# Eight of the sixteen gate tiles moved from the softmax loop to the linear attention

## The reference

```python
def mixer(z, w_in, ...):
    h = z @ w_in
    (q_a, k_a, v_a, r_a, lr_f, lr_b, q_b, k_b, v_b, g_a, g_b) = jnp.split(h, SPLIT_POINTS, axis=-1)
    a = gla_branch(q_a, k_a, v_a, r_a, lr_f, lr_b, ...)      # linear attention, 4 heads
    b = attention_branch(q_b, k_b, v_b, ...)                 # softmax attention, 8 heads
    y = (jax.nn.sigmoid(g_a + b_merge[0]) * (a @ w_pa)
         + jax.nn.sigmoid(g_b + b_merge[1]) * (b @ w_pb))
    return y @ w_out

# inside gla_branch, forward and on the flipped sequence, in chunks of 64 tokens:
    att = jnp.where(mask, jnp.einsum('bhnid,bhnjd->bhnij', q_dec, k_inv), 0.0)
    o_intra = jnp.einsum('bhnij,bhnjv->bhniv', att, vc)
    kv_chunk = jnp.einsum('bhnjd,bhnjv->bhndv', k_end, vc)   # state products
    ...                                                      # S = decay * S + kv_chunk
    o_inter = jnp.einsum('bhnid,bhndv->bhniv', q_dec, S_prev)
    ...
    o = o * lax.rsqrt(jnp.mean(o * o, axis=-1, keepdims=True) + EPS)   # group mean of each head
```

## Time and profile before

| | |
|---|---|
| runs shown | 3025.6 us median of 3 (3020.71 to 3026.71) |
| profiled execution | 3026.42 us, span 3024.6 us |
| PE matmul busy | 2682.4 us (89%), 18120 matmuls |
| PE weight load busy | 2040.7 us (67%) |
| DVE, ACT, POOL busy | 921.7, 911.7, 890.4 us (about 30% each) |
| mean granted TensorE clock | 0.941 |

### The profile page before, as it was taken

How to read it: one execution, slowest core, us unless ns; L and a number is a source line. 1 busy time by engine, 2 the same in 40 slices (tenths; PEclk the granted TensorE clock), 3 DMA queues, 4 the chain that set the end, 5 groups by cost and what they waited for, 6 DMA issues and landing times.

```text
span 3024.6 us, 44882 instructions
## 1 busy us (share of the span) xinstructions
PE 2682.4 (89%) x18120; PEld 2040.7 (67%) x18120; DVE 921.7 (30%) x2251; ACT 911.7 (30%) x1485; POOL 890.4 (29%) x374
## 2 busy tenths in 40 slices
PE   5999999699999999969998689999878687999996
PEld 3997667699999766769998644444447584444443
DVE  2211432622121143252206433323223613323322
ACT  3431263244344225314434212112113521122111
POOL 2782001367778400136776200000014340000000
PEclk8999997899999999879999899999988988999998
DMA  6543311244644432114555579999962155999994
GB/s 174 179 160 123 126 56 56 73 151 150 199 145 157 146 111 84 56 56 140 171 164 155 197 289 421 421 421 421 421 219 103 56 190 232 421 421 421 421 421 183
DMA packets 269403, 643.89 MB, mean 213 GB/s; under 512 B 16544, under 2 KB 188576, under 8 KB 219856
## 3 DMA queue, kind: packets, MB, share of 16 engines
q1 hardware_dynamic: 267664, 635.60, 56.0%
q0 software_dynamic: 1600, 6.29, 0.9%
HBM read 637.66 MB, written 4.19 MB: 212 GB/s over the span
## 4 chain that ended last, share of the span: by engine, by line
PE 76%; DMA 11%; DVE 9%; ACT 2%; issue 1%; SPq 0%; POOL 0%; DVEq 0%; ACTq 0%
PE bank L528 35%; PE bank L492 15%; DMA wring<-in_exp_w 10%; PE bank L983 6%; PE bank L968 5%; PE bank L992 3%; PE bank L944 3%; PE bank L957 3%; PE bank L778 2%; PE bank L560 2%; PE bank L695 1%; PE bank L502 1%; DVE ARENA L1705 1%; DMA bias_table<-ARENA 1%; DVE ARENA_rounded L1501 1%
## 5 line engine op out<-in xcount | busy, mean ns | idle before, releaser
L1760 POOL TENSOR_TENSOR wring_rounded<-wring,wring_rounded 128x1024 fp32r<-128x1024 f32 (+1 forms) x336 | 860.6, 2564 | 480.0 <-ACT wring_rounded L1058 458.3
L528 PE MATMUL bank<-SQ_rounded,wring_rounded 128*128 128x272 f32 (+1 forms) x3456 | 657.7, 290 | 44.1 <-POOL wring_rounded L1760 22.8
L528 PEld LDWEIGHTS bank<-SQ_rounded,wring_rounded 128*128 128x128 f32 x3456 | 548.5, 191 | 49.2 <-issue 37.4
L1058 ACT ACTIVATE wring_rounded<-wring 128x1024 fp32r<-128x1024 f32 (+1 forms) x336 | 375.1, 1119 | 493.5 <-PE bank L528 488.6
L528 PE MATMUL bank<-ARENA_rounded,wring_rounded 128*128 128x272 f32 (+1 forms) x3456 | 448.4, 293 | 57.7 <-DVE ARENA_rounded L1491 27.2
L528 PE MATMUL bank<-XN_rounded,wring_rounded 128*128 128x272 f32 (+1 forms) x1728 | 499.0, 289 | 0.0
L528 PEld LDWEIGHTS bank<-ARENA_rounded,wring_rounded 128*128 128x128 f32 x3456 | 445.6, 194 | 60.8 <-DVE ARENA_rounded L1491 28.5
L528 PEld LDWEIGHTS bank<-XN_rounded,wring_rounded 128*128 128x128 f32 x1728 | 330.4, 191 | 0.0
L983 PE MATMUL bank<-wring,ARENA 128*32 128x512 f32 x2048 | 248.0, 602 | 42.3 <-DVE ARENA L1705 30.2
L1274 ACT ACTIVATE ARENA<-bank 128x512 f32<-128x512 f32 x128 | 76.5, 597 | 660.9 <-PE bank L983 660.9
L492 PE MATMUL bank<-XN,wring 128*128 128x272 f32 (+2 forms) x1088 | 259.2, 403 | 11.8 <-DVE XN L1344 11.8
(11 more groups left out here) (231 smaller groups left out, 2365.1 us busy)
## 6 DMA issues: line engine op xcount, KB each, us to landing
wring<-in_exp_w SPq DMA_DIRECT2D x256, 1024.0 KB, 18.5
ARENA<-in_exp_w SPq DMA_DIRECT2D x128, 1024.0 KB, 17.2
wring<-in_ffn_w_gate SPq DMA_DIRECT2D x44, 1024.0 KB, 5.4
wring<-in_ffn_w_up SPq DMA_DIRECT2D x44, 1024.0 KB, 8.1
wring<-in_ffn_w_down SPq DMA_DIRECT2D x32, 1408.0 KB, 6.2
wring<-in_w_in SPq DMA_DIRECT2D x16, 2048.0 KB, 7.9
wring<-in_conv_w_in SPq DMA_DIRECT2D x24, 512.0 KB, 5.3
wring<-in_attn_w_in SPq DMA_DIRECT2D x5, 2048.0 KB, 7.9
```

Source lines behind the costliest of these rows:

```text
L528: ins = nc.tensor.matmul(o, rounded(a_[:, k, cols]), rounded(x), start=(start and k == 0 and j == 0), stop=(stop and k == len(tiles) - 1 a ...
L1058: st.done(A(rounded(high), w_, ACT.Copy), wh_ready)
L1760: st.done(nc.gpsimd.tensor_tensor(rounded(low), low, part(high), ALU.subtract), wl_ready)
```

## The change

Eight gate tiles stay in the softmax loop, at the steps with n % 3 == 0. Gate tiles 8, 9 and 10 are formed after the state products and before the outputs; tiles 11 to 14 each follow the outputs of one head; tile 15 comes last, ahead of the merge. The group mean of a head follows its gate tile instead of standing after all four outputs. The banks are dealt out anew: state products in 0 to 3, outputs in 4, 5, 0 and 1, group means in 2 and 3, gate tiles in 6 and 7 throughout. ACT follows the same order; its first three high parts of the merge's weights now come after the last gate tile. ACT frees the bank of a group mean after its root.

```diff
-GATE_STEPS = [n for n in range(24) if n % 3 != 2]
+GATE_STEPS = [n for n in range(24) if n % 3 == 0]
+O_BANK = (4, 5, 0, 1)
...
 # tensor program, mixer
-                        b = 6 + half if d == 0 else half
+                        b = 2 * d + half
...
-                for b in (3, 4, 5, 6, 7, 0, 1):
+                for g in range(8, 11):
+                    gate_tile(l, g)
+                for b in range(6):
                     claim(b)
+
+                def group_mean(h):
+                    st.need(sq_ready)
+                    products(2 + h % 2, "act", "act", [[(bank[2 + h % 2][:, 0:T], const("mean128"), SQ[:, h, :])]])
+
                 for h in range(4):
...
-                    st.done(ins, bank_full["act"][2 + h])
-                    held[2 + h] = "dve"
-                for h in range(4):
-                    b = (0, 1, 6, 7)[h]
-                    st.need(sq_ready)
-                    products(b, "act", None, [[(bank[b][:, 0:T], const("mean128"), SQ[:, h, :])]])
+                    st.done(ins, bank_full["act"][O_BANK[h]])
+                    held[O_BANK[h]] = "dve"
+                    gate_tile(l, 11 + h)
+                    group_mean(h)
+                gate_tile(l, 15)
...
 # scalar program, mixer
+                for g in range(8, 11):
+                    gate_tile(l, g)
+                for h in range(4):
+                    st.need(bank_full["act"][O_BANK[h]])
+                    st.done(A(SQ[:, h, :], bank[O_BANK[h]][:, 0:T], ACT.Square), sq_ready)
+                    gate_tile(l, 11 + h)
+                    deviation(SQ[:, 4 + h, :], 2 + h % 2, "eps_rms", T, a2d)
+                    mark(bank_free["act"][2 + h % 2])
+                gate_tile(l, 15)
                 for _ in range(HIGHS):
                     high_part()
-                for h in range(4):
-                    st.need(bank_full["act"][2 + h])
-                    st.done(A(SQ[:, h, :], bank[2 + h][:, 0:T], ACT.Square), sq_ready)
-                for h in range(4):
-                    deviation(SQ[:, 4 + h, :], (0, 1, 6, 7)[h], "eps_rms", T, a2d)
...
 # vector program, mixer
-                        b, q = (6 + s // 2, s % 2) if d == 0 else (s // 2, s % 2)
+                        b, q = 2 * d + s // 2, s % 2
...
-                    then(STT(AT[:, h, :], bank[2 + h][:, 0:T], g, SQ[:, 4 + h, :], ALU.mult, ALU.mult),
-                         bank_free["dve"][2 + h])
+                    then(STT(AT[:, h, :], bank[O_BANK[h]][:, 0:T], g, SQ[:, 4 + h, :], ALU.mult, ALU.mult),
+                         bank_free["dve"][O_BANK[h]])
```

More of the change, by code:

```diff
@@ L764, in mixer @@
                         r0, t, at = 64 * (c % 2), c // 2, c * 64
-                        o = bank[2 + h][:, at:at + 64]
+                        o = bank[O_BANK[h]][:, at:at + 64]
                         for d in range(2):
@@ L770, in mixer @@
                             by_row[hp].append((o, ST[hp:hp + 64, 1, 2 - c, tile], QD[hp:hp + 64, 1, h // 2, at:at + 64]))
-                    o = bank[2 + h][:, SEQ:T]
+                    o = bank[O_BANK[h]][:, SEQ:T]
                     for d in range(2):
@@ L774, in mixer @@
                     by_row[hp].append((o, ST[hp:hp + 64, 1, 3, tile], QD[hp:hp + 64, 1, h // 2, SEQ:T]))
-                    claim(2 + h)
                     for r0 in (0, 64):
```

## The result

| | before | after |
|---|---|---|
| median | 3025.66 us (3020.71 to 3029.72, 7 runs) | 3039.36 us (3031.03 to 3042.07, 7 runs) |
| profiled execution, span | 3026.42, 3024.6 us | 3042.07, 3040.3 us |
| mean granted clock | 0.941 | 0.936 |

The ratio is 1.004, 95% interval 1.0026 to 1.0054: 13.7 us slower, where 28.5 us faster was forecast. The seven runs of the kernel after spread over 11 us, those of the kernel before over 9. The profile of the kernel after is of its slowest run.

A forecast was written before the change was run, and what follows sets the result against it. PE was taken to bound the kernel. Each layer gains 30.9 - 0.5 us in the loop and adds 16.4 or 15.9 after it; 28.5 us in all gives 2997 us by the median, own range 2985 to 3009, whole range 2976 to 3019.

The forecast's parts named there:

- Taken out of the loop: Softmax loop: eight gate tiles fewer save 30.9 us a layer, less 0.5; period 9.4 us, still bound by PE.
- The bound I put on the loop: Softmax loop: new stalls of nothing up to 0.5 us in each of 8 periods, 4 us a layer.
- the 0.5 that I had allowed: Softmax loop: the loss to new stalls actually taken into the forecast, 0.5 us a layer.
- Rival C: Softmax loop: thinned of dense work, it loses its clock, 4.4 us in each of 8 periods; 3068 us, chance 0.08.
- Three tiles ahead of the outputs: After the state products: 14.1 us for three tiles begun at half clock, covering the 2.8 us wait for DVE's recurrence.
- Outputs, tile, mean: Four heads after the loop: 5.6 us outputs, 5.0 tile, 0.6 mean, 11.2 us a head, 44.8 for four.
- Rivals A and B: Four heads' outputs and tiles: A full clock throughout, 2980 us, chance 0.15; B outputs at half clock, 3017 us, 0.15.
- The wait ahead of the merge: After tile 15: PE waits 4.2 us for the first chunk of merge weights; bounds 1.7 (DVE only) and 5.5.
- my sign for being right: After tile 15: a wait of about 4 us put down to POOL L1760 would show the forecast right.
- From the merge on: Merge and after: all as before, with the same cold start.

The follow-up runs named there:

- early high parts: The kernel after, with ACT's first three high parts moved ahead of the sigmoid of gate tile 15: 3040.15 us, ratio 1.005 to the kernel before.
- late copies: The kernel after, with ACT's two copies of a finished head pair one step later in its loop: 3008.11 us, ratio 0.9941 to the kernel before.
- n % 3 == 1: The kernel after, with its eight loop gate tiles at these steps in place of n % 3 == 0: 3001.54 us, ratio 0.9929 to the kernel before.
- nine in loop: The kernel after, with loop tiles at n % 3 == 1 plus a ninth at step 0, and two ahead of the outputs: 2983.72 us.
- spread high parts: The kernel after, with loop tiles at n % 3 == 1 and ACT's three high parts after the root of head 2: 2988.93 us.
- all together: The kernel after, with nine loop tiles, one ahead of the outputs, four behind heads, two last, high parts after head 2's root: 2975.4 us.

## Why the prediction was wrong

**Taken out of the loop: the step that failed.** I wrote that the longest chain between the engines is "that of ACT after a gate tile", some 3 us against 3.7, and "so I see no new stall". For five steps of six that is right: without the copies in the way the period is 9.36 us, the 9.4 of the forecast, and DVE and ACT do not become the bound. It left out ACT's copies of a finished pair, which stand in the same program between the exponential and the sigmoid. With them the chain is 5.6 us from the end of the tile to the exponential, and 6.4 to the scores product, against 3.7 us of work that PE has there. The bound I put on the loop, 4 us a layer, was far too narrow. The waits alone are 3 x 2.66 = 8.0 us a layer; the rest is nearly all work at half clock. Counted with 3.86 us for each tile that left, the first layer lost 4.3 us up to the end of the tile at step 3, 20.3 in the six periods behind it (8.0 of them waiting) and 3.9 from there to the end of the state products, the second layer 4.6, 18.6 and 0.5; less the 0.5 that I had allowed, these are the 28 and 23. Most of the 3.9 comes from a fall of the clock at 477.3: the scores of the chunks took 4.75 us where the kernel before took 3.19.

**Rival C had the price and not the mechanism.** I gave it 0.08 and 4.4 us for a period in which the clock falls. Measured, a period with a wait is 13.3 to 13.5 us against 9.36 (16.0 once, where its own tile began at half clock), some 4.1 us, of which 2.66 are the wait and up to 1.4 the slow products; the tile behind it, begun at half clock, then adds 1.4 to 3.0 to the next period. I had the clock fall because the loop is thin. In the kernel after, leaving out the start, it fell eight times inside the two loops: six times near the end of one of the six waits, from 1.0 us before it to 0.3 behind it (as at 412.5 and 1190.7 in the windows above), once without a wait (450.0), and once among the loop's last products (477.3). The kernel with early high parts has the same loop, and its clock fell six times, all near the end of its six waits, so twelve waits of twelve had a fall. With eight or nine tiles and no waits (late copies, n % 3 == 1, nine in loop, spread high parts, all together) it fell once in ten loops, with four tiles twice in two. So the waits did most of it and thinness a little. That it is the waits that bring down the clock rests on this count, in kernels that differ in little else, not on a kernel with the wait alone.

**The start.** I did not see that tile 1 is what brings the clock back up after PE's first wait. In the kernel after the clock stood at 0.50 for 17.1 us there, before for 6.8. Over all the kernels here the clock was up 3.9 to 5.4 us after the end of that wait where step 1 has a tile, 8.5 and 10.7 where the next tile is at step 2, and 12.0 to 14.6 where it is at step 3.

**Three tiles ahead of the outputs:** 12.4 and 11.2 us against 14.1. Right in kind, and DVE's recurrence was covered; in the second layer the clock was still up.

**Outputs, tile, mean:** forecast 5.6 + 5.0 + 0.6 = 11.2 us a head, measured 10.6 for the third (4.62 + 5.45 + 0.56 from start to start, 527.09 to 537.72); the four took 43.8 and 42.1 us against 44.8. The outputs run at 0.128 us a matmul, the weight load's figure of the earlier trace rows, and keep full clock to about their end: behind the second, third and fourth head of the first layer the clock fell at 521.7, 532.0 and 542.2, up to 0.6 us after the tile had begun, and the tile pays for it (in the first head it fell within the outputs, at 508.1). Rivals A and B were both wrong here.

**The wait ahead of the merge:** forecast 4.2, measured 4.25 in both layers, for the wrong reason. I had put it down to the chunk and given DVE's chain 1.7 us. It is DVE's chain, so my sign for being right, a wait put down to POOL, failed too: its last pass takes 2.59 us beside POOL, which the early and the spread high parts showed from both sides. Without POOL it is 2.1. I had named this only as an upper bound.

**From the merge on** little changed, as forecast: 1.6 us less in the first layer, none in the second. What would have warned me was in reach. I read ACT's load from the windows, 56 us of 92 in the earlier trace rows, and nothing in a window says in which order that work stands; the timeline of ACT before had the exponential 5.6 us behind the tile, under a tile that I was taking away.

## What to carry to other kernels

Before taking cover out of a pipelined loop, walk each engine's program over the loop's whole period, here six steps and not three, and ask of each item that stands in it only sometimes what queues behind it. A cover counts by its place, not by its amount: the same eight tiles one step later are worth 38 us, by the waits that are gone and by a start that is at full clock sooner, and a tile in a wait that exists anyway is free. Where a new wait is possible in a loop at full clock, price the half clock behind it together with the wait: here it cost more than the wait itself.

## What the runs showed of the hardware

A DVE pass over two SBUF operands of 128x272 took 0.44 us alone and up to 2.59 us while POOL made a low part (128x1024); a pass with one operand in PSUM kept its 0.44 us beside POOL (L1506 at 559.30 in the kernel after, with POOL at work from 553.47 to 560.69). The products of a head's outputs, 64-row, 128-column weight tiles with 64 columns or 16, took 0.128 us each at full clock and 0.211 at half, not twice as long. With four tiles in the loop, 11 us of small products stood between two tiles, and the clock was 1.00 over most of them, where the outputs of the linear attention, also without a pause, stood at 0.50 for 30 us.
